# In-place multiplies, a statistic one tile later and two weight splits moved forward in a two-layer hybrid diffusion block

## The chip, the cores and the metric

The kernel runs on one core of a Trainium2 chip. TensorE multiplies matrices, VectorE and ScalarE work on tiles that lie in on-chip memory or in the accumulators, GpSimd works on tiles too and issues some of the DMAs, and SyncE's queue issues the loads of the weights. Rows of the profile call them PE (PEld for its weight loads), DVE, ACT, POOL and SP. The metric is the device time of one execution in microseconds, lower is better.

## The reference, cut to what matters

Two layers over 512 latent and 256 context tokens of width 1024. What the change touches is the projection stage with its normalised compressed vectors (`cq`, `ckv`) and the output projection with its residual.

```python
h = modulate(x, sh1, sc1)                      # rms(x) * (1 + scale) + shift
z = h @ p['w_in']                              # na, mla, sg and gqa parts
cq, ckv, k_rope = jnp.split(z_mla, [256, 256 + 192], axis=-1)
q  = (rms(cq)  * p['mla_cq_norm'])  @ p['mla_w_uq']
kv = (rms(ckv) * p['mla_ckv_norm']) @ p['mla_w_ukv']
...
y = 0
for i, o in enumerate(branches):
    y = y + jax.nn.sigmoid(h @ p['w_gate'][i] + p['b_gate'][i]) * (o @ p['w_branch'][i])
x = x + g1[:, None] * (y @ p['w_out'])
x = x + g2[:, None] * conv_ffn(modulate(x, sh2, sc2), p)
```

Layer 0 works on 768 tokens (latent and context), layer 1 computes the context only where latent tokens read it, so most of its tiles are 512 wide.

## The kernel before

All activations are stored feature by token: a tile is 128 features by 768 (or 512) tokens. Each matrix is cut into blocks of 128x1024 values, and each fp32 product is done as three products of rounded parts: `W_hi` with `H_hi`, `W_hi` with `H_lo`, `W_lo` with `H_hi` (`F_hi`, `F_lo` for inputs other than the normalised state). So for each weight block SP loads it into one of two `W_st` slots, ACT rounds it to `W_hi` (function `used`, `split_hi`) and DVE subtracts to get `W_lo` (`split_lo`). Both may start only when PE has finished the block that used the slot before, which PE tells by the semaphore `block_done`; so while PE works on block b+1, ACT and DVE must find the time to split block b+2. An output tile takes eight steps of six matmuls (in 768-wide tiles) or three (in 512-wide ones).

The order on each engine is written by hand; each engine runs its own list in order, and semaphores tie the lists together.

**Projection stage (`in_stage`).** One list, `events()`, is walked by PE, ACT and DVE alike. `g(t)` is the product of tile t: 0 and 1 hold `ckv` (the 32 key-rope rows `kr` sit in tile 1 too), 2 is `gk`, 3 and 4 are `cq`, 5 and 6 are `gq`, 7 on are products of the compressed vectors. At `g(t)` ACT copies the product out of the accumulators into `RAW[t % 4]`, squares it into one of two buffers `SQ`, and splits the next weights (`used`); DVE subtracts for those weights. `s(i)` is the statistic of item i (0 `ckv`, 1 `kr`, 2 `gk`, 3 `cq`, 4 and 5 `gq`): PE sums squares with a small matmul that is put between the steps of the next tile (after step 3 if one is due; after step 2 and step 7 in `gk` if two are due), ACT makes a first estimate of the reciprocal root and its square, DVE does one Newton step in two operations and multiplies the raw tile by gain and root. For `ckv` and `cq`, both of two pieces, DVE writes the result to the scratch tile `TT`, ACT rounds it to `F_hi`, DVE subtracts to get `F_lo`, and only then is the second piece multiplied, as `TT` is one buffer. Items with rotary positions end with a shuffle on DVE into `TT` and three operations on POOL (`rotate`).

**Output phase (`out_tiles`).** PE does steps 1 to 7 of output tile 0, steps 1 to 3 of tile 1, the last step of tile 0 (the last input is made late), then the last five steps of tile 1. During that time POOL's DMA `x_head` brings the residual rows back into `XY`, where the merge phase had put its result. Per tile DVE adds gate times product to the residual (`out_add`), ACT squares the new row for the next norm, and both then split the weights two blocks on. Tile 2 uses the accumulators of tile 0 (a `pair`), so PE waits for `out_add` of tile 0 before it, and for the weights.

Of the kernel before, what the change touches and what calls it, by code (L numbers as in the profile page):

```python
# [232 lines left out]
def events():  # L233

    g, s = (lambda t: ("gemm", t)), (lambda i: ("stat", i))
    return [g(0), g(1), s(0), s(1), g(2), g(3), s(2), g(4), s(3), g(5), s(4), g(6), g(7), g(8), s(5), s(6), g(9),
            s(7), g(10), s(8), s(9), ("values", 0), g(11), g(12), s(10), s(11), g(13), s(12), g(14), g(15), g(16),
            s(13), s(14), ("gates", 0), s(15)]


def z_after(its, i):

    return sum(x.z for x in its[:i + 1])


def last_item(its, t):
    return max(i for i, x in enumerate(its) if any(src[0] == t for src in x.src))
# [34 lines left out]
def hybrid_backbone_kernel(nc, x_in, cc_in, cb_in, w_ada, w_mod, w_all, par, sg_gain, sg_ws, sg_bs, bias_na, mask_na,  # L282
# [3 lines left out]
    with es:  # L286
# [116 lines left out]
        def dest(it):  # L403
            r0, r1 = it.rows
            if it.to in ("cq", "ckv"):
                return TT
# [603 lines left out]
        def _(act):  # L1010
# [46 lines left out]
            def in_stage(l, ph):  # L1057
# [15 lines left out]

                for what, t in events():
# [16 lines left out]
                    if what == "gemm":  # L1091
                        x = tiles[t]
                        if x.last:
                            act.wait_ge(S["block_done"], b0 + x.visit + 1)
                        else:
                            subs += 1
                            act.wait_ge(S["sub_gemm"], base["sub_gemm"] + subs)
                        if t >= 4:
                            act.wait_ge(S["in_zn"], base["in_zn"] + z_after(its, last_item(its, t - 4)))
                        op(RAW[t % 4][0:x.rows, 0:x.w], pair(turn(t) % 3)[0:x.rows, 0:x.w], ACT.Copy  # L1100
                           ).then_inc(S["in_raw"], 1)
                        act.wait_ge(S["in_raw"], base["in_raw"] + t + 1)
# [23 lines left out]
                    if it.to in ("cq", "ckv"):  # L1126
                        for q, (_, s0, s1, _) in enumerate(it.src):
                            n_hi += 1
                            act.wait_ge(S["in_zn"], base["in_zn"] + z_after(its, t - 1) + q + 1)
                            op(F_hi[s0:s1, 1 + n_hi, 0:it.w], TT[s0:s1, 0:it.w], ACT.Copy).then_inc(S["in_hi"], 1)  # L1130
# [124 lines left out]
            def out_tiles(w, name, last_phase=False, squares=False):  # L1255
# [3 lines left out]
                def body(i, final):  # L1259
                    for u in range(2):  # L1260
                        if squares:
# [4 lines left out]
                        used(i, 2, b0 + u, stop=final)  # L1266
# [46 lines left out]
            for l in range(DEPTH):  # L1313
# [10 lines left out]
                out_tiles(w, "out_add", squares=True)  # L1324
# [7 lines left out]
        def _(dve):  # L1332
# [90 lines left out]
            def in_stage(l, ph):  # L1423
# [3 lines left out]
                for what, t in events():  # L1427
# [14 lines left out]
                    for q, (tile, s0, s1, _) in enumerate(it.src):  # L1442
                        src, d = RAW[tile % 4], dest(it) if it.to != "mk" else None
                        gain = PAR[s0:s1, it.gain + q:it.gain + q + 1]
                        if it.to in ("cq", "ckv"):

                            wait(dve, "in_lo", base["in_lo"] + n_lo)
                            wait(dve, "rope_step", base["rope_step"] + 3 * n_rope)
                            stt(TT[s0:s1, 0:it.w], src[s0:s1, 0:it.w], gain, RT[s0:s1, 0:it.w], ALU.mult, ALU.mult
                                ).then_inc(S["in_zn"], 1)  # L1450
                            z += 1
                            n_lo += 1
                            dve.wait_ge(S["in_hi"], base["in_hi"] + n_lo)
                            sub(F_lo[s0:s1, 1 + n_lo, 0:it.w], TT[s0:s1, 0:it.w], F_hi[s0:s1, 1 + n_lo, 0:it.w]
                                ).then_inc(S["in_lo"], 1)
# [13 lines left out]
                        else:  # L1469
                            stt(d[:, 0:it.w], src[r0:r1, 0:it.w], gain, RT[r0:r1, 0:it.w], ALU.mult, ALU.mult  # L1470
                                ).then_inc(S["in_zn"], 1)
                            z += 1
                    if it.rope is not None:
# [3 lines left out]
                        wait(dve, "in_lo", base["in_lo"] + n_lo)  # L1477
# [176 lines left out]
            def out_tiles(w, gate, name, last_phase=False, squares=False, reloads=0):  # L1654
# [3 lines left out]
                def body(i, final):  # L1658
                    for u in range(2):
                        dve.wait_ge(S["block_done"], i * 2 + (b0 + u + 1))  # L1660
                        if reloads and not first(i):
                            dve.wait_ge(S["x_reloaded"], 16 * reloads)
# [16 lines left out]
                        used(i, 2, b0 + u, stop=final and last_phase)  # L1679
# [56 lines left out]
            for l in range(DEPTH):  # L1736
# [18 lines left out]
                dve.wait_ge(S["x_head"], 16 * (l + 1))  # L1755
# [132 lines left out]
```

## Time and profile before

| | before |
|---|---|
| median of 3 runs | 2422.13 us (2419.07 to 2424.84) |
| the profiled execution | 2430.79 us, its span 2429.1 us |
| PE busy | 2300.4 us, 95% of the span |
| DVE, ACT, POOL busy | 1338.9, 955.9, 163.4 us |
| granted TensorE clock, mean | 0.979 |

The span runs from the first to the last instruction of the profiled execution. Busy time of PE includes the time in which it ran at half clock, so a stretch can be busy and slow. Times in rows count from the start of the span.

### The profile page before, as it was taken

What the parts mean: (1) busy time and instruction counts of PE and PEld (TensorE: products, weight loads), DVE (VectorE), ACT (ScalarE), POOL (GpSimd) and SP (SyncE); (2) the same over time, 40 slices, a digit from 0 to 9 for tenths busy, and PEclk for the clock granted to TensorE, in tenths of its full rate; (3) what the DMA queues carried; (4) which work ended last, traced back from release to release, by engine and by line L of the source; (5) the groups of instructions that cost most, each with busy time, mean ns of one, the idle gap of its engine ahead of it and who ended that gap; (6) DMA issues with size and microseconds to landing.
All of it is one profiled execution on the core that took longest, in us unless ns stands there. A gap on an engine that the chain in (4) does not pass through costs nothing.

```text
span 2429.1 us, 34904 instructions
## 1 busy us (share of the span) xinstructions
PE 2300.4 (95%) x12816; PEld 1905.6 (78%) x12816; DVE 1338.9 (55%) x1877; ACT 955.9 (39%) x1389; POOL 163.4 (7%) x169
## 2 busy tenths in 40 slices
PE   6999988999999989999999978999999997999999
PEld 5778766788888868888888866776778885888887
DVE  6555566566667355425524555546745564645555
ACT  3555556422223253213313354545643333433333
POOL 2113010000000000000000001220100000000000
PEclk9999999999999999999999989999999998999999
DMA  7112110243443211111111131120135542222323
GB/s 277 44 53 70 36 39 19 97 146 132 136 135 126 96 52 61 61 61 64 66 61 61 61 123 52 61 70 18 48 115 174 177 164 98 88 98 95 100 95 114
DMA packets 58621, 221.21 MB, mean 91 GB/s; under 512 B 6720, under 2 KB 6720, under 8 KB 57872
## 3 DMA queue, kind: packets, MB, share of 16 engines
q1 hardware_dynamic: 44496, 160.46, 19.5%
q0 software_dynamic: 14016, 59.26, 7.1%
q8 instruction: 72, 1.18, 0.2%
q14 instruction: 37, 0.30, 0.0%
HBM read 214.45 MB, written 5.24 MB: 90 GB/s over the span
## 4 chain that ended last, share of the span: by engine, by line
PE 86%; DVE 5%; ACT 4%; issue 3%; DMA 2%; ACTq 0%; SPq 0%; DVEq 0%
PE PS L586 84%; PE PS L863 3%; ACT TM L1015 1%; ACT XY L1015 1%; DVE F_lo L1337 1%; DVE XY L1340 1%; ACT W_hi L1015 1%; DVE ROPE L1393 1%; ACT F_hi L1015 1%; DMA ROPE<-w_mod 1%; DVE W_lo L1337 0%; DVE TM L1340 0%; DMA SGX<-sg_bs 0%; DMA XY<-x_in 0%; DMA XY<-x_spill 0%
## 5 line engine op out<-in xcount | busy, mean ns | idle before, releaser
L586 PE MATMUL PS<-H_hi,W_hi 128*128 128x512 f32 x2240 | 681.0, 361 | 49.4 <-DVE H_lo L1337 25.6
L586 PE MATMUL PS<-H_lo,W_hi 128*128 128x512 f32 x2240 | 671.8, 357 | 0.0
L586 PE MATMUL PS<-H_hi,W_lo 128*128 128x512 f32 x2240 | 669.3, 356 | 0.0
L1337 DVE TENSOR_TENSOR W_lo<-W_st,W_hi 128x1024 fp32r<-128x1024 f32 x278 | 344.8, 1242 | 547.9 <-ACT W_hi L1015 546.1
L1015 ACT ACTIVATE W_hi<-W_st 128x1024 fp32r<-128x1024 f32 x278 | 293.4, 1056 | 808.9 <-PE PS L586 799.4
L586 PEld LDWEIGHTS PS<-H_hi,W_hi 128*128 128x128 f32 x2240 | 369.9, 190 | 124.7 <-issue 44.4
L586 PEld LDWEIGHTS PS<-H_hi,W_lo 128*128 128x128 f32 x2240 | 369.6, 190 | 63.8
L586 PEld LDWEIGHTS PS<-H_lo,W_hi 128*128 128x128 f32 x2240 | 369.6, 190 | 63.5 <-issue 2.2
L586 PE MATMUL PS<-F_hi,W_hi 128*128 128x512 f32 (+1 forms) x952 | 290.2, 359 | 22.6 <-DVE W_lo L1337 11.1
L586 PE MATMUL PS<-F_lo,W_hi 128*128 128x512 f32 (+1 forms) x952 | 288.4, 357 | 0.0
L586 PE MATMUL PS<-F_hi,W_lo 128*128 128x512 f32 (+1 forms) x952 | 288.1, 357 | 0.0
L586 PEld LDWEIGHTS PS<-F_hi,W_hi 128*128 128x128 f32 x952 | 157.9, 190 | 57.5 <-issue 22.6
L1340 DVE SCALAR_TENSOR_TENSOR RA<-PS,PAR,RA 128x511 f32<-128x511 f32 (+1 forms) x264 | 173.9, 659 | 14.6 <-DVE RA L1340 4.6
L586 PEld LDWEIGHTS PS<-F_hi,W_lo 128*128 128x128 f32 x952 | 158.2, 190 | 26.9
L586 PEld LDWEIGHTS PS<-F_lo,W_hi 128*128 128x128 f32 x952 | 157.9, 190 | 26.1
L1340 DVE SCALAR_TENSOR_TENSOR XY<-PS,MOD,XY 128x512 f32 (+1 forms) x96 | 60.6, 658 | 211.7 <-PE PS L586 196.0
L1015 ACT ACTIVATE TM<-PS 128x512 f32<-128x512 f32 (+4 forms) x136 | 83.8, 617 | 113.4 <-PE PS L863 95.2
L1015 ACT ACTIVATE RA<-PS,PAR 128x768 f32<-128x768 f32 (+1 forms) x152 | 126.2, 830 | 0.0
L1015 ACT ACTIVATE XY<-PS,SM 128x768 f32<-128x768 f32 (+3 forms) x122 | 95.3, 783 | 63.5 <-PE PS L586 53.5
L1015 ACT ACTIVATE TM<-XY 128x768 f32<-128x768 f32 (+3 forms) x48 | 37.6, 786 | 149.6 <-DVE XY L1340 131.8
L863 PE MATMUL PS<-MT,XY 128*128 128x128 f32 x432 | 73.5, 289 | 20.6 <-DVE XY L1557 10.0
L863 PEld LDWEIGHTS PS<-MT,XY 128*128 128x128 f32 x432 | 47.1, 143 | 50.7 <-issue 32.2
(130 smaller groups left out, 2102.8 us busy)
## 6 DMA issues: line engine op xcount, KB each, us to landing
W_st<-w_all SPq DMA_DIRECT2D x278, 512.0 KB, 3.4
RA<-w_mod POOLq DMA_DIRECT2D x40, 512.0 KB, 3.6
TM<-w_mod POOLq DMA_DIRECT2D x40, 512.0 KB, 3.7
RA<-w_ada SPq DMA_DIRECT2D x8, 512.0 KB, 8.8
XY<-bias_na POOLq DMA_DIRECT2D x2, 1792.0 KB, 8.0
RA<-w_mod SPq DMA_DIRECT2D x6, 512.0 KB, 8.3
XY<-x_in SPq DMA_DIRECT2D x4, 768.0 KB, 11.5
x_spill<-XY POOLq DMA_DIRECT2D x1, 3072.0 KB, 11.2
```

Of the source, the lines that this page charges most:

```text
L586: return nc.tensor.matmul(o, lhsT, rhs, start=start, stop=stop)
L863: ins = nc.tensor.transpose(b[:, P * (t - first):P * (t - first) + P], p[:, P * (t % nk):P * (t % nk) + P], MT[:, M_ID, :])
L1015: return nc.scalar.activation(o, i, func, **kw)
L1337: return nc.vector.tensor_tensor(o, a, b, f)
L1340: return nc.vector.scalar_tensor_tensor(o, a, s, b, f0, f1)
L1393: nc.vector.tensor_tensor_reduce(SCALE_P, SCALE_W[j % 3], CB[c], 1.0, 0.0, ALU.mult, ALU.add, MOD[:, c, SC1 + j:SC1 + j + 1]).then_inc(S[" ...
```

## The change

Three edits, in code that both layers run.

1. The pieces of `cq` and `ckv` are multiplied by gain and root in place, in `RAW`, not into `TT`; both multiplies of an item come first, and the two subtractions for `F_lo` after them. ACT rounds from `RAW`. Since a `RAW` buffer is now read until `F_lo` is made, the copy of tile t+4 waits for `in_lo` of tile t where t is a `cq` or `ckv` tile. The shuffle and the multiplies no longer wait for `in_lo`.
2. In `events()` the statistic `s(1)` (`kr`) comes after `g(2)` and not before it. PE thus puts statistic 0 after step 3 of `gk` and statistic 1 after step 3 of tile 3.
3. In the first pair of tiles of the output phase the next weights are split before the residual work: ACT splits before the square, DVE splits and then waits for `x_head`, which was the first wait of the phase.

```diff
-    return [g(0), g(1), s(0), s(1), g(2), g(3), s(2), g(4), s(3), g(5), s(4), g(6), g(7), g(8), s(5), s(6), g(9),
+    return [g(0), g(1), s(0), g(2), s(1), g(3), s(2), g(4), s(3), g(5), s(4), g(6), g(7), g(8), s(5), s(6), g(9),
...
+                        if t - 4 in split:
+                            act.wait_ge(S["in_lo"], base["in_lo"] + split.index(t - 4) + 1)
...
-                            op(F_hi[s0:s1, 1 + n_hi, 0:it.w], TT[s0:s1, 0:it.w], ACT.Copy).then_inc(S["in_hi"], 1)
+                            op(F_hi[s0:s1, 1 + n_hi, 0:it.w], RAW[tile % 4][s0:s1, 0:it.w], ACT.Copy).then_inc(S["in_hi"], 1)
...
                     for u in range(2):
+                        early = reloads and first(i)
+                        if early:
+                            used(i, 2, b0 + u)
                         if squares:
...
-                        used(i, 2, b0 + u, stop=final)
+                        if not early:
+                            used(i, 2, b0 + u, stop=final)
...
-                            wait(dve, "in_lo", base["in_lo"] + n_lo)
-                            wait(dve, "rope_step", base["rope_step"] + 3 * n_rope)
-                            stt(TT[s0:s1, 0:it.w], src[s0:s1, 0:it.w], gain, RT[s0:s1, 0:it.w], ALU.mult, ALU.mult
+                            stt(src[s0:s1, 0:it.w], src[s0:s1, 0:it.w], gain, RT[s0:s1, 0:it.w], ALU.mult, ALU.mult
                                 ).then_inc(S["in_zn"], 1)
                             z += 1
-                            n_lo += 1
-                            dve.wait_ge(S["in_hi"], base["in_hi"] + n_lo)
-                            sub(F_lo[s0:s1, 1 + n_lo, 0:it.w], TT[s0:s1, 0:it.w], F_hi[s0:s1, 1 + n_lo, 0:it.w]
-                                ).then_inc(S["in_lo"], 1)
...
+                    if it.to in ("cq", "ckv"):
+                        for tile, s0, s1, _ in it.src:
+                            n_lo += 1
+                            dve.wait_ge(S["in_hi"], base["in_hi"] + n_lo)
+                            sub(F_lo[s0:s1, 1 + n_lo, 0:it.w], RAW[tile % 4][s0:s1, 0:it.w],
+                                F_hi[s0:s1, 1 + n_lo, 0:it.w]).then_inc(S["in_lo"], 1)
...
                         dve.wait_ge(S["block_done"], i * 2 + (b0 + u + 1))
+                        if early:
+                            used(i, 2, b0 + u)
+                            if u == 0:
+                                dve.wait_ge(S["x_head"], 16 * reloads)
...
-                dve.wait_ge(S["x_head"], 16 * (l + 1))
```

The first place is DVE in the projection stage of layer 0, from the Newton step of `ckv` to the weights behind the shuffle of `kr`. Before:

```order
L1340 SCALAR_TENSOR_TENSOR XY<-PS,XY 128x768
L1340 SCALAR_TENSOR_TENSOR XY<-XY 128x768
L1340 SCALAR_TENSOR_TENSOR TM<-TM,PAR,XY 128x768
L1337 TENSOR_TENSOR F_lo<-TM,F_hi 128x768
L1340 SCALAR_TENSOR_TENSOR TM<-TM,PAR,XY 64x768
L1337 TENSOR_TENSOR F_lo<-TM,F_hi 64x768
L1340 SCALAR_TENSOR_TENSOR XY<-PS,XY 32x768
L1340 SCALAR_TENSOR_TENSOR XY<-XY 32x768
L1340 SCALAR_TENSOR_TENSOR FA<-TM,PAR,XY 32x768
L1479 STREAM_SHUFFLE TM<-FA 32x512
L1337 TENSOR_TENSOR W_lo<-W_st,W_hi 128x1024 x2
```

The third and fifth rows are the two multiplies of `ckv`, with a subtraction between them, and both weight subtractions (for the blocks of tiles 4 and 5) come after the shuffle. The same stretch of DVE now:

```order
L1346 SCALAR_TENSOR_TENSOR XY<-PS,XY 128x768
L1346 SCALAR_TENSOR_TENSOR XY<-XY 128x768
L1346 SCALAR_TENSOR_TENSOR TM<-TM,PAR,XY 128x768
L1346 SCALAR_TENSOR_TENSOR TM<-TM,PAR,XY 64x768
L1343 TENSOR_TENSOR F_lo<-TM,F_hi 128x768
L1343 TENSOR_TENSOR F_lo<-TM,F_hi 64x768
L1343 TENSOR_TENSOR W_lo<-W_st,W_hi 128x1024
L1346 SCALAR_TENSOR_TENSOR XY<-PS,XY 32x768
L1346 SCALAR_TENSOR_TENSOR XY<-XY 32x768
L1346 SCALAR_TENSOR_TENSOR FA<-TM,PAR,XY 32x768
L1484 STREAM_SHUFFLE TM<-FA 32x512
L1343 TENSOR_TENSOR W_lo<-W_st,W_hi 128x1024
```

The multiplies stand next to each other, and the weight subtraction of tile 4 has moved ahead of the four operations of `kr`.

On ACT at the same place (names as above; the first row is the first estimate for `ckv`), before:

```order
L1015 ACTIVATE XY<-PS,SM 128x768
L1015 ACTIVATE XY<-XY 128x768
L1015 ACTIVATE F_hi<-TM 128x768
L1015 ACTIVATE F_hi<-TM 64x768
L1015 ACTIVATE XY<-PS,SM 32x768
L1015 ACTIVATE XY<-XY 32x768
L1015 ACTIVATE XY<-PS 128x768
L1015 ACTIVATE TM<-XY 128x768
L1015 ACTIVATE W_hi<-W_st 128x1024
```

The copy and the square of `gk` (rows seven and eight) and the weights for tile 4 wait behind the estimate for `kr`. Now:

```order
L1013 ACTIVATE XY<-PS,SM 128x768
L1013 ACTIVATE XY<-XY 128x768
L1013 ACTIVATE F_hi<-TM 128x768
L1013 ACTIVATE F_hi<-TM 64x768
L1013 ACTIVATE XY<-PS 128x768
L1013 ACTIVATE TM<-XY 128x768
L1013 ACTIVATE W_hi<-W_st 128x1024
L1013 ACTIVATE XY<-PS,SM 32x768
L1013 ACTIVATE XY<-XY 32x768
```

The estimate for `kr` and its square moved behind the weights.

The last place is the start of layer 0's output phase. Here the lists name the semaphores, and the rows are DVE's, before:

```order
L1372 TENSOR_SCALAR MOD<-MOD 128x2x8
L1340 SCALAR_TENSOR_TENSOR XY<-PS,MOD,XY 128x512 [waits mod_step,x_head,block_done,phase_act,phase_pe]
L1340 SCALAR_TENSOR_TENSOR XY<-PS,MOD,XY 128x256
L1337 TENSOR_TENSOR W_lo<-W_st,W_hi 128x1024 [waits w_hi,block_done]
L1340 SCALAR_TENSOR_TENSOR XY<-PS,MOD,XY 128x512 [waits block_done]
```

The weight subtraction stands behind the residual addition, which waits for `x_head`. Now:

```order
L1378 TENSOR_SCALAR MOD<-MOD 128x2x8
L1343 TENSOR_TENSOR W_lo<-W_st,W_hi 128x1024 [waits mod_step,block_done,w_hi,phase_act,phase_pe]
L1346 SCALAR_TENSOR_TENSOR XY<-PS,MOD,XY 128x512 [waits x_head]
L1346 SCALAR_TENSOR_TENSOR XY<-PS,MOD,XY 128x256
L1343 TENSOR_TENSOR W_lo<-W_st,W_hi 128x1024 [waits w_hi,block_done]
```

The subtraction is ahead of the wait for `x_head`, and ACT's list has `W_hi` ahead of the square in the same way.

## Rows read from the trace of the kernel before

**Rows 1.** Timeline, PE: start, duration, work, [idle before <- releaser], at six pauses

```profile
100.07 0.59 PE L586 MATMUL PS<-H_hi,W_hi 128*128 128x512 f32 x2 [1.06 <-issue]
...
125.92 1.34 PE L586 MATMUL PS<-TM,MT 128*128 128x512 f32 x3 [1.97 <-ACT TM L1015]
...
800.82 1.00 PE L586 MATMUL PS<-F_hi,W_hi 128*128 128x512 f32 x2 [3.55 <-DVE W_lo L1337]
...
1489.84 0.77 PE L586 MATMUL PS<-H_hi,W_hi 128*128 128x512 f32 x1 [3.86 <-ACT W_hi L1015]
...
1512.32 1.39 PE L586 MATMUL PS<-TM,MT 128*128 128x512 f32 x2 [3.31 <-ACT TM L1015]
...
2012.81 0.79 PE L586 MATMUL PS<-F_hi,W_hi 128*128 128x512 f32 x1 [5.17 <-DVE W_lo L1337]
```

**Rows 2.** Windows: stretch, length, PE, PEld, DVE, ACT, POOL busy (x), PEclk, DMA share, GB/s

```profile
100.00:110.00 10.00, 9.93 (x53) 8.40 (x54) 4.97 (x6) 3.47 (x5) 4.49 (x3) 1.00 0.32 107
126.00:136.00 10.00, 10.00 (x44) 8.02 (x44) 4.89 (x6) 4.18 (x5) 2.62 (x3) 0.83 0.17 52
801.00:811.00 10.00, 10.00 (x43) 8.63 (x44) 2.81 (x4) 1.79 (x2) 0.00 (x0) 0.73 0.32 107
1490.00:1500.00 10.00, 10.00 (x30) 7.33 (x31) 3.71 (x3) 1.94 (x3) 4.36 (x3) 0.70 0.32 107
2013.00:2023.00 10.00, 10.00 (x34) 7.99 (x35) 2.94 (x5) 2.36 (x4) 0.00 (x0) 0.74 0.30 107
880.00:1360.00 480.00, 478.77 (x2730) 416.49 (x2729) 223.66 (x294) 132.03 (x140) 0.00 (x0) 1.00 0.19 63
```

**Rows 3.** Timeline, PE in output tile 2 of layer 0, two steps' parts

```profile
802.26 0.84 PE L586 MATMUL PS<-F_hi,W_lo 128*128 128x512 f32 x2
802.90 0.63 PE L586 MATMUL PS<-F_hi,W_hi 128*128 128x512 f32 x1
```

**Rows 4.** Chain of waits: start, length, work (here the merge phase of layer 0)

```profile
1005.82 66.80 PE PS L586 x384
```

**Rows 5.** Timeline, DVE and ACT, projection stage of layer 0

```profile
98.75 1.23 DVE L1337 TENSOR_TENSOR W_lo<-W_st,W_hi 128x1024 fp32r<-128x1024 f32 x1
...
119.47 1.02 DVE L1340 SCALAR_TENSOR_TENSOR TM<-XY,PAR 128x768 f32<-128x768 f32 x1
...
122.40 1.02 DVE L1340 SCALAR_TENSOR_TENSOR TM<-TM,PAR,XY 128x768 f32<-128x768 f32 x1
...
125.03 0.84 ACT L1015 ACTIVATE TM<-TM 128x768 f32<-128x768 f32 x1
```

**Rows 6.** Timeline, ACT (two rows), then DVE, projection stage of layer 1

```profile
1482.07 0.85 ACT L1015 ACTIVATE F_hi<-TM 64x768 fp32r<-64x768 f32 x1 [2.07 <-DVE TM L1340]
...
1486.33 1.04 ACT L1015 ACTIVATE W_hi<-W_st 128x1024 fp32r<-128x1024 f32 x1
...
1507.53 0.75 DVE L1340 SCALAR_TENSOR_TENSOR TM<-XY,PAR 128x512 f32<-128x512 f32 x1
...
1509.70 0.75 DVE L1340 SCALAR_TENSOR_TENSOR TM<-TM,PAR,XY 128x512 f32<-128x512 f32 x1
```

**Rows 7.** Timeline, DVE and POOL side by side, the same stage of layer 1

```profile
1502.12 2.28 DVE L1337 TENSOR_TENSOR W_lo<-W_st,W_hi 128x1024 fp32r<-128x1024 f32 x1
...
1505.68 1.81 DVE L1340 SCALAR_TENSOR_TENSOR XY<-XY 128x512 f32<-128x512 f32 x1
...
1505.66 1.29 POOL L511 TENSOR_TENSOR RA<-RA,TM 128x512 f32<-128x512 f32 x1
```

**Rows 8.** Timeline, DVE, the first residual additions of both output phases

```profile
796.20 1.14 DVE L1340 SCALAR_TENSOR_TENSOR XY<-PS,MOD,XY 128x512 f32<-128x512 f32 x2 [8.60 <-DMA XY<-x_in]
...
2008.80 0.75 DVE L1340 SCALAR_TENSOR_TENSOR XY<-PS,MOD,XY 128x512 f32<-128x512 f32 x1 [7.10 <-DMA XY<-x_spill]
```

**Rows 9.** Page, DMA issues: out<-in, engine, count, KB each, us to landing

```profile
W_st<-w_all SPq DMA_DIRECT2D x278, 512.0 KB, 3.4
XY<-x_in POOLq DMA_DIRECT2D x1, 2688.0 KB, 9.4
```

More of the change, by code:

```diff
@@ L404, in dest @@
             r0, r1 = it.rows
-            if it.to in ("cq", "ckv"):
-                return TT
             if it.to == "kr":
@@ L1072, in square @@
                         squares += 1
+                split = [src[0] for it in its if it.to in ("cq", "ckv") for src in it.src]
                 for what, t in events():
@@ L1126, in in_stage @@
                     if it.to in ("cq", "ckv"):
-                        for q, (_, s0, s1, _) in enumerate(it.src):
+                        for q, (tile, s0, s1, _) in enumerate(it.src):
                             n_hi += 1
                             act.wait_ge(S["in_zn"], base["in_zn"] + z_after(its, t - 1) + q + 1)
-                            op(F_hi[s0:s1, 1 + n_hi, 0:it.w], TT[s0:s1, 0:it.w], ACT.Copy).then_inc(S["in_hi"], 1)
+                            op(F_hi[s0:s1, 1 + n_hi, 0:it.w], RAW[tile % 4][s0:s1, 0:it.w], ACT.Copy).then_inc(S["in_hi"], 1)
                 def store_nv(n, tbs):
@@ L1253, in merge, with out_tiles @@
                 base.advance(**MERGE_COUNTS)
-            def out_tiles(w, name, last_phase=False, squares=False):
+            def out_tiles(w, name, last_phase=False, squares=False, reloads=0):
                 b0 = done[0]
@@ L1323, in _ @@
                 begin(act, p0 + PH_OUT, "pe", "dve")
-                out_tiles(w, "out_add", squares=True)
+                out_tiles(w, "out_add", squares=True, reloads=l + 1)
                 end(act, "act")
@@ L1442, in in_stage @@
                     for q, (tile, s0, s1, _) in enumerate(it.src):
-                        src, d = RAW[tile % 4], dest(it) if it.to != "mk" else None
+                        src, d = RAW[tile % 4], dest(it) if it.to not in ("mk", "cq", "ckv") else None
                         gain = PAR[s0:s1, it.gain + q:it.gain + q + 1]
                         if it.to in ("cq", "ckv"):
-                            wait(dve, "in_lo", base["in_lo"] + n_lo)
-                            wait(dve, "rope_step", base["rope_step"] + 3 * n_rope)
-                            stt(TT[s0:s1, 0:it.w], src[s0:s1, 0:it.w], gain, RT[s0:s1, 0:it.w], ALU.mult, ALU.mult
+                            stt(src[s0:s1, 0:it.w], src[s0:s1, 0:it.w], gain, RT[s0:s1, 0:it.w], ALU.mult, ALU.mult
                                 ).then_inc(S["in_zn"], 1)
                             z += 1
-                            n_lo += 1
-                            dve.wait_ge(S["in_hi"], base["in_hi"] + n_lo)
-                            sub(F_lo[s0:s1, 1 + n_lo, 0:it.w], TT[s0:s1, 0:it.w], F_hi[s0:s1, 1 + n_lo, 0:it.w]
-                                ).then_inc(S["in_lo"], 1)
                         elif it.to in ("nq", "nk"):
@@ L1476, in in_stage @@
                         dl, s = rope_operands(it)
-                        wait(dve, "in_lo", base["in_lo"] + n_lo)
                         wait(dve, "rope_step", base["rope_step"] + 3 * n_rope)
@@ L1659, in body @@
                     for u in range(2):
+                        early = reloads and first(i)
                         dve.wait_ge(S["block_done"], i * 2 + (b0 + u + 1))
+                        if early:
+                            used(i, 2, b0 + u)
+                            if u == 0:
+                                dve.wait_ge(S["x_head"], 16 * reloads)
                         if reloads and not first(i):
@@ L1678, in body @@
                                 tt(TT[:, 0:w], TT[:, 0:w], SQ[1][:, 0:w], ALU.add).then_inc(S["sq_sum"], 1)
-                        used(i, 2, b0 + u, stop=final and last_phase)
+                        if not early:
+                            used(i, 2, b0 + u, stop=final and last_phase)
                 def last(i):
```

## The prediction

> **What bounds the kernel now.** PE is busy for 2300.4 of 2429.1 us, so almost nothing that the change does to ACT or DVE counts unless it moves a moment at which PE stands still. I read the timeline of PE for its pauses first. Six of them lie where the change works [rows 1]: in the projection stage 1.06 and 1.97 us in layer 0, 3.86 and 3.31 us in layer 1; at the start of the output phase 3.55 us in layer 0 and 5.17 us in layer 1. Together 18.9 us. The bracket names what ended each: weights (W_hi, W_lo) or a square that the statistic needs (TM).
>
> Second, the granted clock behind each pause [rows 2]. Behind 1.06 us it stays at 1.00, the 2.4 GHz level. Behind four of the others the means over ten microseconds are 0.83, 0.73, 0.70 and 0.74; as the lower level is 0.50 (1.2 GHz), the half-clock stretch is twenty times what is missing to 1: 3.4 us behind 1.97, 5.4 behind 3.55, 6.0 behind 3.86, 5.2 behind 5.17. At half clock one part of a step (a 512 and a 256 wide matmul) takes 802.90 - 802.26 = 0.64 us [rows 3]; at full clock 384 matmuls take 66.80 us, 0.348 us for two [rows 4]. So a stretch at half clock loses 45% of itself. A pause that goes gives back its own length and that.
>
> **Part 1, in-place multiply.** No operation is added. In layer 0 the second multiply of `cq` starts at 122.40; the first ends at 119.47 + 1.02 = 120.49 [rows 5]. With no scratch tile between them it follows at once: 1.9 us earlier, and the second F_hi, the copy and the square of tile 5 behind it on ACT, which ends at 125.03 + 0.84 = 125.87, too. That square ended PE's pause of 1.97 us. Left is about 0.1 us, and the clock should stay up: 1.9 + 0.45 x 3.4 = 3.4 us. In layer 1 the same distance is 1509.70 - (1507.53 + 0.75) = 1.4 us [rows 6]. That alone cuts the 3.31 us pause to 1.9 us, by the row of layer 0 still long enough to drop the clock.
>
> The new wait of ACT (tile t+4's copy for `in_lo` of tile t) stands ahead of that copy, the square and the weights behind it, with PE's statistic waiting for them. The awaited subtraction is now two DVE operations behind the multiplies, one `g` or more earlier in the list than the copy, so I take 0; the most it could cost is one subtraction, some 1 us by the multiply's duration.
>
> **Part 2, the statistic of `kr` later.** In layer 0 the pause of 1.06 us ended when the W_lo that starts at 98.75 was done (99.98, PE at 100.07: a hand-over of 0.1 us) [rows 5]. That subtraction stood behind `kr`'s Newton step, multiply and shuffle; now it stands ahead of them. The pause goes: 1.06 us, no clock to win. In layer 1 the W_hi for tile 4 starts at 1486.33 [rows 6]. It moves forward by two ACT operations of `kr` (0.85 us each by the square in rows 5, so 1.7) and by 1.9 us of part 1 (`ckv` is 768 wide in both layers), and back by one step of PE, three parts of 0.35, as statistic 0 now comes after step 3: 1486.33 - 1.7 - 1.9 + 1.05 = 1483.8. W_hi 1.04 and W_lo 1.23 end it at 1486.1. PE is done with tile 3 at 1489.84 - 3.86 = 1485.98. A pause of 0.2 us remains: gain 3.6 us and 0.45 x 6.0 = 2.7 us of clock, 6.3 us.
>
> That step of delay also reaches the weights of tile 3, which ACT splits behind the `kr` square. PE shows no pause worth a row there; cost 0, at most 1.05 us a layer.
>
> The second pause of layer 1 is the term that I know least. `kr`'s shuffle now comes later relative to PE, while PE, at full clock, comes sooner, so POOL's rotations of `kr` and then `gk` fall on DVE's work for `gk` and `cq`. [rows 7] show what an overlap costs: a W_lo of 2.28 instead of 1.23 us, and a 512 wide Newton operation of 1.81 us which starts with a POOL operation of 1.29 us and ends 0.5 us behind it. So each overlap costs DVE about 1.1 us. Without any, even the one that is there now would go: 1.4 + 1.1 = 2.5 us of the 3.31, the pause falls under 1.06 us and the clock stays up, a gain near 4 us. With three new ones, 1.4 - 3.3 = -1.9 us. I take 0: I expect one or two.
>
> The Trainium skill, page SBUF — State Buffer, section "SBUF: two separate sides", calls the port pair that GpSimd shares with VectorE "an exclusive lock, not a bandwidth split", held for a whole instruction. The rows agree with it in kind (the blocked operation waits the other out); taken strictly it points to the -1.9 end here, with the sum at 2403.6.
>
> **Part 3, output phase.** Before, the split of tile 2's weights stood behind the residual addition, that behind the DMA. The five last steps of tile 1 are 5 x 3 x 0.35 = 5.2 us in layer 0, and PE finishes them at 800.82 - 3.55 = 797.27. So tile 0 was done at 792.0, and ACT and DVE need 1.04 + 1.23 and two hand-overs: W_lo is ready at 794.5, well ahead. What is late next is the accumulator of tile 0: its residual addition starts at 796.20, when x_in has landed, and ends at 797.34 [rows 8]. PE starts at 797.45: pause 0.2, not 3.55. Gain 3.3 us and 0.45 x 5.4 = 2.4, 5.7 us. In layer 1 the steps before are shorter, PE ends at 2012.81 - 5.17 = 2007.64 and the addition at 2008.80 + 0.75 = 2009.55. Pause 2.0 us: gain 3.1 us, and of the clock only the difference, 0.45 x (5.2 - 3.4) = 0.8 us, as 1.97 us was enough for a fall. 3.9 us.
>
> The moved split also moves a DMA: SP's load two blocks on is released 6 us earlier, while the residual is still coming in. If its 512 KB took their full share from a transfer that moves 2688 KB in 9.4 us [rows 9], the residual would come 1.8 us later in each layer. But the load is issued at about 794.6 and the residual lands at 796.2, and a load takes 3.4 us to land alone, of which 1.8 are bytes at that rate; its packets barely meet the residual's. I take 0, and 1.8 us each for the range. Tile 3's weights on ACT now wait for the first square, but have all of tile 2, 24 x 0.35 = 8.3 us.
>
> The same page of the Trainium skill, same section, warns of a DMA issued from GpSimd: while VectorE holds the shared pair, GpSimd "cannot write the descriptors". The residual's DMA is one, and the W_lo subtraction now runs during it; the trace before has none there to compare. By that rule the residual would land up to 1.2 us later in each layer, and the time would be 2404.
>
> **The sum.** Layer 0 projection 1.06 + 3.4 = 4.5; layer 1 projection 6.3 + 0; output phases 5.7 and 3.9. Together 20.4 us. Everything behind these places waits for PE's progress and shifts with it. The profiled execution took 2430.79 us, 8.7 us over the median; it becomes 2410.4, and the median 2422.13 - 20.4 = 2401.7.
>
> **Rivals.**
> A, contention eats a part (POOL on DVE in layer 1, the weight load or the lock on the residual's DMA in both output phases). For it: rows 7, and transfers that do overlap in time. Against: the dates above. Price: 1.9 us, twice 1.8 us, and 1.5 us because layer 0's output pause then reaches 2.0 us and drops the clock: 20.4 - 7.0 = 13.4 us, 2408.7.
> B, more comes back: no overlap with POOL (4 us) and a pause of 2.0 us that leaves the clock up in layer 1's output phase (1.5 us). For: the pause is at the edge. Time 2422.1 - 25.9 = 2396.2.
> C, the change does not do what it says: the pauses only move, because the residual and the POOL chain end last anyway and half-clock stretches follow as before. Then the layer 0 projection (1.06 + 1.9) is all that is sure: 2419.2. Against it: the dates of the residual leave 3.4 and 3.2 us in plain sight.
> D, slower: the full clock in the long stretches is kept only because PE pauses now and then, and with pauses gone the chip grants 1.2 GHz somewhere in the merge or feed-forward phases. Each microsecond there loses 0.45; to undo 20.4 us and end 0.2% behind takes 56 us at half clock, from which point this case decides; the time would be 2427 or more. Against: 480 us of nearly unbroken work at 1.00 [rows 2].
>
> **How the numbers follow.** 0.2% is 4.8 us, about what a measurement of this kernel can tell from no change. Forecast 0.60, A 0.20, B 0.10, C 0.07, D 0.03. Forecast, A and B are faster by more than that, C is within it, D beyond it on the other side: 0.90, 0.07, 0.03. The range has to hold the forecast, A and B with a spread of some 3 us, as the three runs have: 2393 to 2412.
>
> **What would show it.** PE's pauses at the four marked places: in layer 0 none over 0.5 us, in layer 1 one of some 3 us before the statistic of tile 5 and one of 2.0 us before output tile 2, with the residual's addition as its releaser. The clock at 1.00 behind all pauses of layer 0. Two multiplies side by side on DVE. If output tile 2 of layer 0 still waits, the DMA is the cause, and its landing date tells; if PE busy time falls by less than 7 us, the clock did not come back.

## The result and the profile after

| | before | changed |
|---|---|---|
| median | 2421.47 us (4 runs) | 2395.9 us (4 runs, 2389.42 to 2398.22) |
| ratio, 95% interval | | 0.9891 (0.9871 to 0.9912) |
| a second measurement, as after_again | 2416.78 us (11 runs) | 2395.7 us (6 runs), 0.9907 (0.9880 to 0.9934) |
| span of the profiled execution | 2429.1 us | 2396.6 us |
| PE busy | 2300.4 us | 2281.2 us |

The change is faster by 1.1%, 25.6 us between the medians of the first measurement and 21.1 us in the second; the forecast was 20.4 us and 2401.7 us, with 2393 to 2412 as its range. On the page of the changed kernel PE is as busy a share of a shorter span, and the busy time of DVE and ACT is unchanged to the microsecond (1338.9 and 955.9 before):

```profile
span 2396.6 us, 34895 instructions
...
PE 2281.2 (95%) x12816; PEld 1894.9 (79%) x12816; DVE 1339.3 (56%) x1877; ACT 956.8 (40%) x1389; POOL 164.6 (7%) x169
```

Of the six pauses of [rows 1] two are left. In PE's timeline of the changed kernel (start, duration, work, idle before it and what ended that) they are the one before the statistic of tile 5 in layer 1 and the one before output tile 2 of layer 1:

```profile
1489.02 0.70 PE L584 MATMUL PS<-TM,MT 128*128 128x512 f32 x1 [3.15 <-ACT TM L1013]
...
1982.73 0.50 PE L584 MATMUL PS<-F_hi,W_hi 128*128 128x512 f32 x1 [2.21 <-DVE XY L1346]
```

The windows that answer to [rows 2] (stretch, length, busy time of PE, PEld, DVE, ACT and POOL, granted clock, DMA share, GB/s) cover the same places: tiles 4 and 6 of layer 0, its output tiles, tile 4 and then tile 6 of layer 1, and output tile 2 of layer 1.

```profile
100.00:110.00 10.00, 10.00 (x56) 8.38 (x55) 5.67 (x6) 4.61 (x6) 5.68 (x5) 1.00 0.16 52
120.00:130.00 10.00, 10.00 (x53) 8.06 (x53) 5.50 (x7) 5.79 (x8) 1.49 (x2) 1.00 0.17 52
785.00:795.00 10.00, 10.00 (x58) 8.67 (x57) 4.38 (x6) 2.33 (x4) 0.00 (x0) 1.00 0.17 57
...
1463.00:1473.00 10.00, 10.00 (x41) 6.69 (x39) 7.75 (x10) 8.10 (x10) 0.00 (x0) 1.00 0.18 66
...
1489.00:1499.00 10.00, 9.98 (x37) 7.23 (x38) 5.78 (x7) 5.97 (x9) 3.86 (x3) 0.83 0.15 52
...
1983.00:1993.00 10.00, 10.00 (x45) 8.26 (x45) 5.25 (x6) 3.50 (x5) 0.00 (x0) 1.00 0.17 55
```

The clock is at 1.00 (2.4 GHz) in all of them but one. It is lower only behind the 3.15 us pause; behind the 2.21 us pause, where I expected a fall to 1.2 GHz, it stayed up.

What each stretch of the program took shows where the time went. The marks are the starts of PE's instructions in the timelines: from the first product of a layer to its first attention matmul, then the merge phase, the output phase up to the sum of squares, the attention of layer 1. Both projection stages start while the granted clock is still at half, for 2.8 to 5.9 us. All in us:

| kernel | projection 0 | merge 0 | output 0 | projection 1 | attention 1 | output 1 |
|---|---|---|---|---|---|---|
| before | 163.4 | 339.8 | 74.6 | 148.6 | 178.7 | 53.0 |
| before_again | 163.4 | 341.3 | 73.6 | 147.2 | 170.8 | 52.9 |
| changed | 158.7 | 333.5 | 69.2 | 141.7 | 174.8 | 47.6 |
| after_again | 158.3 | 335.0 | 68.5 | 141.9 | 171.7 | 49.1 |
| after_third | 159.7 | 333.4 | 68.3 | 140.9 | 172.0 | 47.4 |
| p1_in_place | 158.7 | 333.4 | 74.4 | 141.9 | 174.3 | 53.1 |
| p2_order | 160.7 | 341.3 | 75.7 | 147.3 | 170.7 | 53.1 |
| p12_projection | 158.8 | 341.3 | 74.7 | 143.9 | 178.9 | 53.2 |
| p3_output_phase | 161.6 | 339.8 | 69.1 | 147.3 | 170.7 | 47.3 |
| p13_without_order | 159.4 | 341.3 | 69.4 | 141.0 | 170.6 | 48.8 |
| pairs_apart | 158.8 | 339.8 | 68.0 | 141.2 | 173.9 | 45.3 |
| late_gk_turn | 158.9 | 339.8 | 68.3 | 136.1 | 173.7 | 47.3 |
| pairs_and_late | 159.8 | 335.0 | 69.1 | 136.2 | 173.5 | 45.2 |
| pairs_late_old_order | 158.5 | 339.8 | 69.1 | 140.4 | 173.2 | 45.3 |

Between the means of the two traces of before and the three of the changed kernel, the four places that the edits touch give 4.5, 5.4, 6.4 and 5.0 us: 21.3 us where 20.4 was forecast. The merge phase of layer 0 gives another 6.6 us and the attention of layer 1 another 1.9 us, and nothing in them was edited.

A stretch can differ between two traces by more than an edit did to it, as the granted clock behind a pause is not the same each time. So each reading below is made of three numbers: the stretch, its pauses (idle time of PE of over 0.15 us), and the time at half clock outside them, which loses 45% of itself. With the pauses and that loss taken off, all fourteen traces have 128.8 to 129.7 us in layer 1's projection stage, 44.4 to 44.6 us in its output phase and 160.9 to 161.3 us in its attention. This is an estimate from the traces' instructions and clock records.

### The profile page after: what moved, and what is told of

It is laid out like the page before. It is cut to its first block, busy times and chain, and to the rows that moved or that the text cites. A ratio compares the mean times of both kernels' runs of the same rounds, so it can differ in the third digit from the quotient of the medians.

```text
span 2396.6 us, 34895 instructions
## 1 busy us (share of the span) xinstructions
PE 2281.2 (95%) x12816; PEld 1894.9 (79%) x12816; DVE 1339.3 (56%) x1877; ACT 956.8 (40%) x1389; POOL 164.6 (7%) x169
## 4 chain that ended last, share of the span: by engine, by line
PE 88%; DVE 4%; ACT 3%; issue 2%; DMA 2%; ACTq 0%; SPq 0%; DVEq 0%
PE PS L584 85%; PE PS L861 3%; ACT TM L1013 1%; DVE F_lo L1343 1%; ACT XY L1013 1%; DVE ROPE L1399 1%; DMA ROPE<-w_mod 1%; ACT F_hi L1013 0%; DVE XY L1346 0%; DVE W_lo L1343 0%; DMA SGX<-sg_bs 0%; ACT W_hi L1013 0%; DMA XY<-x_spill 0%; DVE XY L1562 0%; DVE TM L1346 0%
## 5 line engine op out<-in xcount | busy, mean ns | idle before, releaser
L584 PEld LDWEIGHTS PS<-F_lo,W_hi 128*128 128x128 f32 x952 | 156.8, 188 | 25.6
```

The source lines that it names most:

```text
L584: return nc.tensor.matmul(o, lhsT, rhs, start=start, stop=stop)
```

## The experiments

### One part at a time

p1_in_place keeps the old list and the old output phase:

```diff
-    return [g(0), g(1), s(0), g(2), s(1), g(3), s(2), g(4), s(3), g(5), s(4), ...
+    return [g(0), g(1), s(0), s(1), g(2), g(3), s(2), g(4), s(3), g(5), s(4), ...
...
-                        early = reloads and first(i)
+                        early = False
```

> Only the in-place multiply; order of statistics and output phase as before. Theory (pauses of TensorE and the half clock behind them carry the gain): layer 0 loses the 1.97 us pause and its half-clock stretch, 3.4 us; layer 1's first pause goes from 3.86 to about 2.0 us (1.9 us), the second from 3.31 to 1.9 to 3.3 us, both still with a fall of the clock; together 5 to 8 us. The 1.06 us pause of layer 0 stays. Rival (the part only works together with the moved statistic, since the weights still stand behind kr): under 2 us.

Measured: 0.9958 of before (0.9943 to 0.9972), 10 us. The rival is out. More came than the 5 to 8 us that I expected, though the interval (7 to 14 us) reaches into that, and one thing was wrong: the 1.06 us pause of layer 0 is gone too. Two stretches of DVE's timeline in layer 0, before `kr`'s Newton step and behind its shuffle:

```profile
88.31 1.94 DVE L1346 SCALAR_TENSOR_TENSOR TM<-TM,PAR,XY 128x768 f32<-128x768 f32 x2
90.25 1.87 DVE L1343 TENSOR_TENSOR F_lo<-TM,F_hi 128x768 fp32r<-128x768 f32 x2
...
95.99 0.73 DVE L1484 STREAM_SHUFFLE TM<-FA 32x512 f32<-32x512 f32 x1
96.75 1.23 DVE L1343 TENSOR_TENSOR W_lo<-W_st,W_hi 128x1024 fp32r<-128x1024 f32 x1
```

The two multiplies of `ckv` stand side by side, and the weights for tile 4 start at 96.75, still behind the shuffle, 2.0 us before the 98.75 of [rows 5]. That is enough for a pause of 1.06 us. In layer 1 the pauses are 1.86 and 1.77 us, and PE's timeline at both and the windows behind them are

```profile
1479.67 0.47 PE L584 MATMUL PS<-H_hi,W_hi 128*128 128x512 f32 x1 [1.86 <-issue]
...
1497.73 1.13 PE L584 MATMUL PS<-TM,MT 128*128 128x512 f32 x2 [1.77 <-ACT TM L1013]
```

```profile
1479.67:1489.67 10.00, 10.00 (x40) 7.60 (x41) 5.90 (x7) 4.31 (x6) 5.23 (x4) 1.00 0.32 107
1497.73:1507.73 10.00, 9.99 (x45) 7.44 (x46) 5.70 (x7) 7.52 (x10) 4.29 (x3) 1.00 0.24 72
```

with the clock at 1.00 behind both. So layer 1's stage takes 141.9 us, as long as in the changed kernel (140.9 to 141.9).

p2_order has only the new list:

```diff
-    return [g(0), g(1), s(0), s(1), g(2), g(3), s(2), g(4), s(3), g(5), s(4), ...
+    return [g(0), g(1), s(0), g(2), s(1), g(3), s(2), g(4), s(3), g(5), s(4), ...
```

> Only the statistic of kr one tile later. Theory: the 1.06 us pause of layer 0 goes, the 1.97 us one stays; layer 1's first pause goes from 3.86 to about 2.8 us (1.7 us for the two scalar operations of kr that no longer stand ahead, less 1.05 us for the later first statistic, and up to 1 us more from the same order on VectorE); together 2 to 3 us. Rival (the in-place multiply adds nothing and the order carries all of the projection stage): 9 us or more.

Measured: 0.9988 (0.9973 to 1.0003), the 3 us of the theory, but not clear of nothing at all. Layer 1 tells why it isn't more; PE's timeline at its two pauses, and DVE's at the first multiply of `cq` between them:

```profile
1490.10 0.47 PE L586 MATMUL PS<-H_hi,W_hi 128*128 128x512 f32 x1 [1.84 <-issue]
...
1511.76 1.22 PE L586 MATMUL PS<-TM,MT 128*128 128x512 f32 x1 [5.39 <-ACT TM L1015]
```

```profile
1506.98 0.75 DVE L1340 SCALAR_TENSOR_TENSOR TM<-XY,PAR 128x512 f32<-128x512 f32 x1 [2.65 <-POOL RA L511]
```

The first pause fell from 3.86 to 1.84 us, and the second grew from 3.31 to 5.39 us. What the weights gained, the chain through `cq` did not pass on: PE now comes to the statistic sooner, but the multiply of `cq`, which writes the scratch tile, waits 2.65 us for GpSimd's rotation of `gk`, which reads it. In the kernel before the same multiply starts without a wait (1507.53, [rows 6]), and the in-place multiply of part 1 doesn't need the tile.

p3_output_phase is the kernel before with the output phase of the changed one:

```diff
                     for u in range(2):
+                        early = reloads and first(i)
+                        if early:
+                            used(i, 2, b0 + u)
...
-                dve.wait_ge(S["x_head"], 16 * (l + 1))
```

> Only the weight splits ahead of the residual. Theory: the pauses go from 3.55 and 5.17 to about 0.2 and 2.1 us, with 2.4 us of clock in layer 0 and 0.8 to 2.3 us in layer 1; 9.6 us by the forecast, 10.8 us by the trace of the changed kernel (5.3 and 5.5). Rival (the earlier weight load and the lock on the residual's transfer eat it): under 6 us, with the residual landing over 1 us later than before.

Measured: 0.9954 (0.9937 to 0.9971), 11 us. DVE's timeline in layer 0 and PE's in layer 1:

```profile
791.64 1.22 DVE L1341 TENSOR_TENSOR W_lo<-W_st,W_hi 128x1024 fp32r<-128x1024 f32 x1 [5.74 <-ACT W_hi L1015]
794.12 1.14 DVE L1344 SCALAR_TENSOR_TENSOR XY<-PS,MOD,XY 128x512 f32<-128x512 f32 x2 [1.26 <-DMA XY<-x_in]
...
1994.71 0.50 PE L586 MATMUL PS<-F_hi,W_hi 128*128 128x512 f32 x1 [1.90 <-DVE XY L1344]
```

The subtraction for the weights is done 1.3 us before the residual lands, and what PE waits for in layer 1 is now the residual's addition (XY), not W_lo.

p12_projection is the changed kernel with `early = False` and the old wait for `x_head`:

```diff
-                        early = reloads and first(i)
+                        early = False
...
+                dve.wait_ge(S["x_head"], 16 * (l + 1))
```

> Parts 1 and 2 together, output phase as before. Theory (parts add up over the three places): 10.8 us by the forecast, 11.5 us by the trace of the changed kernel (4.5 and 7.0). The merge phase of layer 0, which no edit touches and which was 6.4 us shorter in the changed kernel's trace, is as long as in either trace by chance. Rival (the change itself shortens the merge phase and the attention of layer 1): 20 us or more, with merge at 333 us.

Measured: 0.9951 (0.9935 to 0.9968), 12 us. With part 3's 11 us that makes 23, the changed kernel's 26 (or 22 to 23 by its second ratio) within the intervals: the parts add up. The merge phase took 341.3 us, so these two parts do not shorten it.

p13_without_order is the changed kernel with the old list:

```diff
-    return [g(0), g(1), s(0), g(2), s(1), g(3), s(2), g(4), s(3), g(5), s(4), ...
+    return [g(0), g(1), s(0), s(1), g(2), g(3), s(2), g(4), s(3), g(5), s(4), ...
```

> The changed kernel with the old order of statistics (parts 1 and 3 without part 2). Theory from the in-place multiply alone (layer 0 without either pause, layer 1 with 1.86 and 1.77 us at full clock, as long as with part 2): the moved statistic is worth nothing once the multiplies are in place, so this takes the time of the changed kernel, 0.989 of before, with 158.7 us to the first attention and about 142 us for layer 1's projection stage. Rival (part 2 carries its own 3 us): 0.9905 of before.

Measured: 0.9911 (0.9889 to 0.9934), 159.4 and 141.0 us for the projection stages against 158.3 to 159.7 and 140.9 to 141.9 us in the three traces with the new list. Beside the in-place multiply, the moved statistic is worth nothing that this run shows. Whether it costs the 0.002 between the ratios they can't tell.

### What holds the two pauses that are left

late_gk_turn moves the shuffle of `gk`, and with it GpSimd's rotations, behind the work on `cq`; the scratch tile is free for it since `cq` is multiplied in place:

```diff
-                    if it.rope is not None:
+                    turned = [] if it.to == "gk" else [its[2], it] if it.to == "cq" else [it]
+                    for it in turned:
+                        if it.rope is None:
+                            continue
```

> The changed kernel with gk's shuffle, and so GpSimd's three rotations of gk, after the multiplies and subtractions of cq. Theory (GpSimd holds up VectorE in layer 1's second pause): the three cq operations take 0.69, 0.75 and 0.75 us instead of 1.08, 1.67 and 1.76, the shuffle no longer waits 1.2 us for kr's rotation, the pause of 3.15 us falls to under 1 us and the clock stays at 1.00: 2.5 to 5 us less than the changed kernel. Rival (the chain through the two scalar copies and the square ends the pause whatever GpSimd does): pause over 2.5 us, no gain; and if gk's rotations now fall on the next tiles' weights, a new pause of 1 to 2 us behind.

Measured: 0.9920 (0.9900 to 0.9939), not faster than the changed kernel as a whole, but the stage did what the theory says: 136.1 us where the changed kernel takes 141.7. First DVE and POOL in the changed kernel (timeline, layer 1, the Newton operation and the two multiplies of `cq`, then gk's rotations on POOL):

```profile
1482.69 1.08 DVE L1346 SCALAR_TENSOR_TENSOR XY<-XY 128x512 f32<-128x512 f32 x1
1483.81 1.67 DVE L1346 SCALAR_TENSOR_TENSOR XY<-XY,PAR 128x512 f32<-128x512 f32 x1
1485.40 1.76 DVE L1346 SCALAR_TENSOR_TENSOR TM<-TM,PAR,XY 128x512 f32<-128x512 f32 x1
...
1481.03 2.19 POOL L506 TENSOR_TENSOR TM<-TM,ROPE 128x512 f32<-128x512 f32 x1 [0.95 <-DVE TM L1484]
1483.17 1.76 POOL L507 TENSOR_TENSOR RA<-RA,ROPE 128x512 f32<-128x512 f32 x1
1485.00 1.60 POOL L509 TENSOR_TENSOR RA<-RA,TM 128x512 f32<-128x512 f32 x1
```

Then the same operations in late_gk_turn, with PE's pause and the window behind it:

```profile
1487.23 0.69 DVE L1346 SCALAR_TENSOR_TENSOR XY<-XY 128x512 f32<-128x512 f32 x1
1487.96 0.75 DVE L1346 SCALAR_TENSOR_TENSOR XY<-XY,PAR 128x512 f32<-128x512 f32 x1
1488.62 0.75 DVE L1346 SCALAR_TENSOR_TENSOR TM<-TM,PAR,XY 128x512 f32<-128x512 f32 x1
...
1491.49 1.28 POOL L506 TENSOR_TENSOR TM<-TM,ROPE 128x512 f32<-128x512 f32 x1 [6.72 <-DVE TM L1486]
```

```profile
1491.24 1.13 PE L584 MATMUL PS<-TM,MT 128*128 128x512 f32 x2 [0.69 <-ACT TM L1013]
```

```profile
1491.20:1501.20 10.00, 9.96 (x45) 7.41 (x46) 7.00 (x8) 7.53 (x10) 8.23 (x5) 1.00 0.25 73
```

Three DVE operations went from 4.5 to 2.2 us, the pause from 3.15 to 0.69 us, and the clock stays at 1.00. The rows agree with the Trainium skill's rule of an exclusive lock between VectorE and GpSimd (page SBUF — State Buffer, section "SBUF: two separate sides"): each side's operation grows by about what is left of the other's.

Not all of the 5.6 us is the edit's. The pause gives 2.5 us and the clock behind it 1.5 us (0.45 x 3.4). The rest is the clock behind a later pause, 2.88 us long in the changed kernel and 2.90 us here, that no edit touches. PE's windows behind it (stretch, length, PE busy, granted clock, DMA share, GB/s), of the changed kernel and then of late_gk_turn:

```profile
1563.70:1573.70 10.00, 9.32 (x29) 0.83 0.29 107
```

```profile
1564.30:1574.30 10.00, 8.98 (x37) 1.00 0.32 107
```

None of it is in the ratio; the merge phase of this kernel took 339.8 us against 333.4, which hides about as much in the trace.

pairs_apart puts output tiles 0 and 1 into the accumulators that the gate products don't use, so that tile 2 doesn't need tile 0's:

```diff
-                        ins = gemm_k(t, w, (b0 + t) % 2, k, k_tiles, F_hi, F_lo)
+                        ins = gemm_k(p + t, w, (b0 + t) % 2, k, k_tiles, F_hi, F_lo)
...
-                        wait(pe, free, i * 2 + (base[free] + u - 1))
+                        if not (p and isinstance(i, int)):
+                            wait(pe, free, i * 2 + (base[free] + u - 1))
...
-                out_tiles(w, KT, "out_add", "y_lo", "gate_sig")
+                out_tiles(w, KT, "out_add", "y_lo", "gate_sig", p=2)
```

> The changed kernel with output tiles 0 and 1 in the two accumulators that no gate product uses, so that tile 2 doesn't wait for the residual's addition. Theory (the residual's landing is what is left in the output phase): the pause of 2.2 us before tile 2 of layer 1 and the 0.1 to 0.2 us of layer 0 go, the next pause over 1 us is that before the norm; 2.2 us less than the changed kernel. Rival (something else, such as the weights or the clock, ends this pause too): no change, pause over 1.5 us with another releaser.

Measured: 0.9908 (0.9886 to 0.9931), and 45.3 us for layer 1's output phase where the changed kernel's traces have 47.4 to 49.1. The pause before tile 2 is gone: this window lies where it would be.

```profile
1984.00:1994.00 10.00, 10.00 (x46) 8.28 (x45) 5.22 (x6) 2.31 (x5) 0.00 (x0) 1.00 0.60 223
```

The residual's landing was thus all that held tile 2. Its 2 us are below what the ratio can tell.

pairs_and_late has both edits.

> Both of the last two. Theory: the two places are independent, 5 to 7 us less than the changed kernel, 0.986 to 0.987 of before. Rival: the unchanged stretches (merge phase of layer 0, attention of layer 1), which moved by up to 8 us between traces of the same code, hide it: no difference outside the interval.

Measured: 2384.79 us, 0.9869 (0.9849 to 0.9889), 2382.74 to 2391.93, with 136.2 and 45.2 us in the two stretches. It has the lowest ratio here, 0.2% (5 us) below the changed kernel's; the medians are 11 us apart, but were measured beside different runs of the kernel before. The intervals of the two ratios overlap, and this kernel's merge phase took 335.0 us, so the traces and not the ratios carry that both places gained.

pairs_late_old_order is this version with the old list, the same edit as in p13_without_order.

> The fastest version so far (accumulators apart, gk's rotation late) with the old order of statistics. Theory (part 2 is worth nothing beside the in-place multiply): layer 0 as before at 158.7 us; in layer 1 the pause before tile 4 comes back at 1.9 us, since the weights stand behind kr again, so 1 to 2 us more than with the new order there, within the interval of 0.987. Rival (kr's rotation then lies earlier and helps cq): 1 us less or better.

Measured: 0.9899 (0.9871 to 0.9928), the projection stage of layer 1 at 140.4 us. PE's timeline at the two places:

```profile
1484.74 0.47 PE L584 MATMUL PS<-H_hi,W_hi 128*128 128x512 f32 x1 [1.91 <-issue]
...
1501.71 0.70 PE L584 MATMUL PS<-TM,MT 128*128 128x512 f32 x1 [0.68 <-ACT TM L1019]
```

With GpSimd out of the way the moved statistic pays: it is what closes the first pause of layer 1, 1.9 us, as expected. The stretches differ by more, 4.2 us, and the rest is clock at places that the edit doesn't touch. The stage began with more time at half clock, which costs about 1 us; PE's windows from its start, of pairs_late_old_order and then of pairs_and_late:

```profile
1444.20:1454.20 10.00, 10.00 (x43) 0.73 0.00 0
```

```profile
1432.80:1442.80 10.00, 10.00 (x49) 0.84 0.00 0
```

And behind the pause of 2.9 us near the end of the stage the clock fell here (0.83 over ten microseconds) and not there (1.00), another 1.5 us.

### Controls

after_again and after_third are the changed kernel, before_again the kernel before, without an edit.

> The changed kernel once more, as a control for the stretches that no edit touches. Theory (their length is set anew in each execution): the projection stages again 158.7 and 141.7 us, the output phases 69.2 and 47.6 us, each within 1.5 us, while the merge phase of layer 0 (333.5 us in the first trace) and the attention of layer 1 (174.8 us) come out elsewhere within 333 to 342 and 170 to 179 us. Rival (the change itself made the merge phase shorter): 333.5 us again.

> The kernel before once more, one look. Theory (the pace of TensorE in the merge phase of layer 0 is drawn anew in each execution): merge phase anywhere from 333 to 342 us, not bound to the 339.8 us of the first trace; the clock behind the 1.97 us pause of layer 0 may stay at 1.00, as it did behind 1.81 us of the same code in another run; the pauses of 3.55 us and more are all followed by a fall. Rival (the pace hangs on the kernel): 339.8 us again, within 0.5.

> The changed kernel a third time, one look. Theory: merge phase of layer 0 anywhere from 333 to 342 us; pause before output tile 2 of layer 1 of 1.9 to 2.2 us, with or without a fall of the clock. Rival (the changed kernel always has the short merge phase, 333.5 and 335.0 us so far): below 336 us again.

after_third and before_again are one execution each, of 2393.8 and 2421.66 us. The four edited places repeat within 1.7 us. The attention of layer 1 does not: 178.7 and 170.8 us for the kernel before, 174.8, 171.7 and 172.0 us for the changed one. The clock accounts for it. The windows over this stretch, of before and then of before_again, have mean clocks of 0.95 and 1.00:

```profile
1596.80:1775.50 178.70, 167.48 (x1379) 0.95 0.11 38
```

```profile
1595.70:1766.60 170.90, 160.52 (x1380) 1.00 0.12 39
```

The merge phase of layer 0 came out at 333.4, 335.0 and 333.4 us in the changed kernel and at 339.8 and 341.3 us before. The 1.5 us within each pair is the clock again, which fell once at the start of the phase in before_again (and in after_again), and not in before:

```profile
441.00:451.00 10.00, 10.00 (x49) 0.83 0.31 107
```

```profile
440.00:450.00 10.00, 10.00 (x58) 1.00 0.31 107
```

What is left are two lengths, 333.4 and 339.8 us. My theory, that each execution draws one anew, is not borne out: both kernels that were traced again kept theirs, and the rival of after_third named just this result. Five traces have the short one (the changed kernel's three, p1_in_place, pairs_and_late), the other nine the long one. p12_projection, p3_output_phase and p13_without_order, which share the parts, are among the nine, so no part carries it; that it hangs on the kernel as a whole is not excluded. Windows from the middle of the phase, of the kernel before and then of the changed one, show what differs (PE busy with its count, clock, DMA share, GB/s):

```profile
516.00:536.00 20.00, 20.00 (x115) 1.00 0.40 132
```

```profile
510.00:530.00 20.00, 20.00 (x117) 1.00 0.37 131
```

The full clock and no pause in both, and 2% more matmuls in the same time. In the timelines each third pair of matmuls takes 0.36 to 0.37 instead of 0.35 us in the slower case. What decides which pace a stretch gets stays open.

## Why the prediction was right, point by point

**The bound.** PE's pauses and the half clock behind them were the right thing to count. The edits that shortened the pauses of a stretch in total shortened the stretch; p2_order, which moved 2 us from one pause to the next in layer 1, left it as it was (147.3 us, 147.2 in before_again). PE, DVE and ACT have the same number of instructions before and after, and the stretches without their pauses and lost clock are the same.

**Part 1.** In layer 0 the 1.97 us pause went, as worked out; with the 1.06 us one the stage gave 4.5 us, the forecast's 4.5. The clock term of 1.5 us in it was a coin's side: behind that pause the unchanged code lost the clock in the traces of before and of before_again, and kept it in those of p2_order and p3_output_phase.

**Part 2.** The 1.06 us pause was put down to it, and either part alone removes it: p1_in_place without part 2, p2_order with it alone. In layer 1 each part alone halves the pause, from 3.86 us to 1.86 by part 1 and to 1.84 by part 2, and both together remove it. I had added both in one line (1486.33 - 1.7 - 1.9 + 1.05), and the sum at that place was right: the pause is gone, 0.2 forecast. The shares were not: part 1's 1.9 us came as worked out, but part 2's 1.7 - 1.05 = 0.65 us measured 2.0 us. I had followed `W_hi`, which the row of the pause names and which was done at 1487.37. The last thing that PE waited for was `W_lo`, behind `kr`'s shuffle on DVE in the kernel before:

```profile
1488.51 3.44 DVE L1337 TENSOR_TENSOR W_lo<-W_st,W_hi 128x1024 fp32r<-128x1024 f32 x2
```

Both parts shorten this same wait, and part 2 does it on DVE as well as on ACT.

**Layer 1's second pause.** I took no gain, with POOL's overlap taking back the 1.4 us. The pause is 3.15 us where 3.31 was: right in size and in cause. Part 1 alone took it to 1.77 us, its 1.4 us as worked out, and late_gk_turn, which moves POOL's rotations away, to 0.69 us with the clock up, the 4 us that I gave for no overlap at all. Alone, part 2 would have made this pause worse (5.39 us, with the wait for the scratch tile), which the forecast, working out both parts in one, did not have to see.

**Part 3.** In layer 0 the gain is 5.4 us (5.7 forecast): the wait for the weights is gone and the residual lands in time. In layer 1 the pause of 2.0 us came out at 2.21, 2.07 and 2.0 us, ended by the residual's addition. The gain is 5.0 us, not 3.9: the mis-sized term is the clock. I took the one 2 us pause of the trace, which had been followed by a fall, for the rule. Behind the 2.21 us pause and that of after_third it stayed at 1.00. Behind that of after_again it fell, and there the gain is 3.9 us, just the forecast's.

**The two costs taken at 0.** The earlier weight load and the subtraction beside GpSimd's DMA did not delay the residual by more than half a microsecond: it lands 9.3 us after its issue in layer 0 (9.4 in [rows 9]) and 8.2 us in layer 1 (7.8 before). The DMA rows of the page of the changed kernel:

```profile
XY<-x_in POOLq DMA_DIRECT2D x1, 2688.0 KB, 9.3
...
XY<-x_spill POOLq DMA_DIRECT2D x1, 1792.0 KB, 8.2
```

The starved descriptors, of which the Trainium skill warns for a DMA from GpSimd (same page and section), do not show here. The subtraction ran from 780.61 in layer 0, some 7 us behind the DMA's issue. The 2404 us that I took from this warning did not follow from the page: it speaks of VectorE operations in a two-port mode and says of `tensor_tensor`, which this subtraction is, that no such stall was seen.

**The rivals.** A did not happen beyond the 0.4 us of layer 1. B did in half: the clock stayed up in two of three traces, GpSimd's overlap remained; that the time, 2395.9, is B's 2396.2 is luck, as B's price for the overlap was not gained. C and D are out: the pauses went, and the long stretches of the changed kernel kept the clock, but for single falls of 3.4 us at the start of a merge phase, which the traces of before have too.

**What the forecast did not have.** The merge phase of layer 0 is 6.6 us shorter in the changed kernel's traces, and it is unexplained. How much of it is in the medians can't be told: they differ by 25.6 and by 21.1 us in the two measurements, and the second one's interval (16 to 29 us) holds the edits' places alone, 21.3 us, as well as these and the merge phase, 27.9 us. The time being within 6 us of the forecast is thus owed to the edits' places; the exact number is not.

## What to carry to other kernels

Count pauses of the bounding engine, name for each the last thing it waits for, and ask of an edit only what it does to that. Two edits that shorten the same wait do not add up: run each alone before giving it a price. When a pause stays, look at what runs beside the operations of its chain, not only at the chain: here three GpSimd operations on the wrong microseconds made a pause 2.5 us longer, 4 us where the clock fell behind it. And before an edit is credited with a shorter stretch, take off the pauses and the half clock at places that it doesn't touch: of 5.6 and 4.2 us in two of these comparisons, 1.5 and 2.5 us were such clock.

## What the runs showed of the hardware

The granted clock behind a pause isn't settled by the pause's length alone. Counted at the edited places and at the untouched pause of 2.9 us near the end of layer 1's projection stage, over all fourteen traces:

| pause | how many | clock fell | stayed at 1.00 |
|---|---|---|---|
| 1.77 to 2.21 us | 16 | 4 (1.81, 1.88, 1.97, 2.07 us) | 12 |
| 2.88 to 2.93 us | 14 | 10 | 4 |
| 3.15 and 3.16 us | 5 | 3 | 2 (after_third, pairs_apart) |
| 3.27 to 5.39 us | 17 | 17 | 0 |

One example with a fall and one without, windows behind the 1.81 us pause of the same code in before_again and in p3_output_phase:

```profile
127.40:137.40 10.00, 10.00 (x43) 7.83 (x44) 4.89 (x6) 4.18 (x5) 2.04 (x2) 0.83 0.17 52
```

```profile
125.70:135.70 10.00, 9.99 (x51) 8.02 (x52) 6.09 (x7) 5.80 (x7) 2.65 (x3) 1.00 0.17 52
```

And PE at full clock has two paces for the same unbroken row of matmuls, 2% apart, which an engineer who compares two traces of a 340 us phase will take for an effect of the edit.
